# Routed experts in a hybrid decoder layer: 50 tiles of whole and half units with bounded gathers and plain scatters, in place of 72 tiles with scatter-adds

## The reference

```python
_, idx = lax.top_k(jnp.where(expert_mask, biased, -jnp.inf), TOP_K)   # 8 experts a token
w = w / jnp.sum(w, axis=-1, keepdims=True) * ROUTED_SCALE
...
def expert(acc, p):
    wg, wu, wd, g = p
    a = jax.nn.silu(t @ wg) * (t @ wu)
    return acc + g[:, None] * (a @ wd), None
```

## Time and profile before

| | |
|---|---|
| time, median of 3 runs (lowest to highest) | 2030.07 us (2028.19 to 2030.41) |
| the profiled execution's own time, and its span | 2028.67 us, 2026.8 us |
| mean granted TensorE clock | 0.968 |
| busy: PE, DVE, ACT, POOL | 93%, 32%, 22%, 20% |
| moved by DMA | 419.35 MB: 339.19 on q1 (SP), 78.10 on q0 (POOL) |

### The profile page before, as it was taken

The page is one execution under the profiler, slowest core; times in us unless marked ns, Lnnn a source line. Parts: engine busy times, 40 slices in busy tenths (PEclk is TensorE's granted clock), DMA queues, the critical chain, the costliest instruction groups (busy, mean ns, idle before and its releaser), DMA issues.

```text
span 2026.8 us, 25917 instructions
## 1 busy us (share of the span) xinstructions
PE 1890.4 (93%) x8348; PEld 1188.2 (59%) x8348; DVE 645.5 (32%) x1571; ACT 445.8 (22%) x946; POOL 411.0 (20%) x661
## 2 busy tenths in 40 slices
PE   5999789989998899999979899999999999999994
PEld 2844467567767668888766444444444444444443
DVE  1215841694269550001266311111111111111114
ACT  1204521452144430000021111111111111111112
POOL 0003420353034100000002322222222222222220
PEclk8999989999999999999978899999999999999997
DMA  9123332111210553210114699999999999999952
GB/s 391 42 83 124 136 126 83 42 45 45 83 43 4 214 204 125 94 72 9 42 41 182 253 371 365 373 367 368 372 363 373 355 381 359 375 367 368 373 165 95
DMA packets 56948, 419.35 MB, mean 207 GB/s; under 512 B 6289, under 2 KB 10001, under 8 KB 31145
## 3 DMA queue, kind: packets, MB, share of 16 engines
q1 hardware_dynamic: 33689, 339.19, 42.0%
q0 software_dynamic: 21456, 78.10, 14.7%
q10 hardware_dynamic: 1728, 1.05, 0.2%
HBM read 362.70 MB, written 55.61 MB: 206 GB/s over the span
## 4 chain that ended last, share of the span: by engine, by line
PE 80%; DVE 9%; ACT 5%; DMA 3%; issue 1%; POOL 1%; SPq 0%; POOLq 0%; DVEq 0%; ACTq 0%
PE ps L1039 25%; PE ps L1061 12%; PE ps L901 10%; PE ps L862 9%; PE ps L847 7%; PE ps L1030 3%; PE ps L933 3%; DVE work L1439 2%; ACT work L585 2%; PE ps L818 2%; ACT work L587 2%; DVE work L1428 1%; DMA Xb<-xT 1%; PE ps L1000 1%; DMA st_out<-work 1%
## 5 line engine op out<-in xcount | busy, mean ns | idle before, releaser
L1039 PE MATMUL ps<-W,work 128*128 128x512 f32 x1168 | 515.2, 594 | 1.6 <-ACT work L1223 1.2
L1039 PEld LDWEIGHTS ps<-W,work 128*128 128x128 f32 x1168 | 216.9, 191 | 247.7 <-issue 247.7
L1061 PE MATMUL ps<-work 128*128 128x512 f32 x576 | 259.1, 592 | 0.0
L1749 DVE SCALAR_TENSOR_TENSOR work<-ps,work 128x256 f32<-128x256 f32 x73 | 35.3, 484 | 515.1 <-ACT work L1229 515.1
L862 PE MATMUL ps<-Hb,W 128*128 128x260 f32 x768 | 172.8, 389 | 0.1
L1061 PEld LDWEIGHTS ps<-work 128*128 128x128 f32 x576 | 103.8, 190 | 103.3 <-issue 103.3
L862 PEld LDWEIGHTS ps<-Hb,W 128*128 128x128 f32 x768 | 148.4, 194 | 23.9 <-ACT work L1123 0.5
L1258 POOL TENSOR_TENSOR work<-work 128x128 f32<-128x128 f32 x168 | 82.8, 525 | 381.2 <-ACT work L587 380.8
L1759 DVE COPY work<-ps 128x512 f32<-128x512 f32 x144 | 99.7, 692 | 178.8 <-DMA ffrows<-work 91.9
L1328 POOL DMA_INDIRECT ffrows<-work x72 | 115.7, 1607 | 195.8 <-DVE work L1759 122.4
L847 PE MATMUL ps<-W,Hb 128*128 128x512 f32 (+1 forms) x320 | 138.4, 592 | 0.0
(11 more groups left out here) (255 smaller groups left out, 2232.1 us busy)
## 6 DMA issues: line engine op xcount, KB each, us to landing
W<-wexp SPq DMA_DIRECT2D x74, 2048.0 KB, 8.7
work<-wexp SPq DMA_DIRECT2D x73, 1024.0 KB, 8.0
W<-wq SPq DMA_DIRECT2D x36, 2048.0 KB, 8.0
work<-st_in SPq DMA_DIRECT2D x8, 1024.0 KB, 9.3
st_out<-work SPq DMA_DIRECT2D x8, 1024.0 KB, 7.5
Xb<-xT SPq DMA_DIRECT2D x2, 2080.0 KB, 18.2
h2rows<-work SPq DMA_DIRECT2D x5, 512.0 KB, 2.6
yT<-Xb SPq DMA_DIRECT2D x2, 1040.0 KB, 5.2
```

Source lines behind the costliest of these rows:

```text
L1039: mm = pe.matmul(ps[:, k % 2, :], xe[:, k % 2, c, :], GU[:, k % 4, c, :], start=(c == 0), stop=(c == KC - 1))
L1061: mm = pe.matmul(ps[:, 4 + hf, :], aT[:, k % 2, f, :], WD[:, k, f, hf * 512:(hf + 1) * 512], start=(f == 0), stop=(f == 1))
```

## The change

The reduction of the experts' results moves from the scatter to the last stage, and tiles can hold two experts.

- *Units.* An expert's slots are cut in units of 64. Two units of one expert are a whole tile; a left-over unit shares a tile with the left-over unit of another expert. The loop goes over pairs of tiles: the first (k = 0) of one expert, the second (k = 1) of two half units, each with its own weights. If there are more whole tiles than mixed ones, the surplus is put in the second list as two halves of one expert. By the counts of the reference's router there are 28 whole tiles and 43 left-over units, so the loop has max(22, (28 + 22) / 2) = 25 rounds, 50 steps, against 72.
- *Matmuls.* For a mixed tile `parts` makes two matmuls of each: 64 columns of stationary data with one expert's weights, and the other 64 with the other's. Transposes are the same.
- *Weights.* Three slots in place of four, one loaded for k = 0, two for k = 1; each is refilled when its own matmuls are done.
- *Gathers and scatters.* Two gather buffers in place of four, and gathers two tiles ahead in place of three. Both DMAs have a bound: rows whose index lies above it (those of empty slots) are not moved. The scatter writes each choice's row to its own place in `yrows` (4160 rows) and adds nothing.
- *Last stage.* For each tile of tokens SP loads 8 rows a token from `yrows` (4 MB a full tile), DVE multiplies each by its gate and adds it (`total`, 8 operations of 128x1024), and the residual (`residual`) comes one tile of tokens later.
- *Routing.* More small DVE operations count units and make two index lists; the gate values are picked after the lists. The shared expert's result stays in SBUF.
- *Merge stage.* `ORDER` puts one product before each state update.

```diff
-            for _ in range(2 if k % 3 == 0 else 1):
-                ORDER.append(decode.pop(0))
-        ORDER += [("N1", 0), ("P", 12), ("S", 0), ("N2", 0)] + [("P", k) for k in range(13, 4 * len(MERGE))]
+            ORDER.append(decode.pop(0))
+        ORDER += [decode.pop(0), ("N1", 0), ("P", 15), ("S", 0), ("N2", 0)] + [("P", k) for k in range(16, 4 * len(MERGE))]
...
             with sp.Fori(1, nq) as i:
-                for k in range(4):
-                    gate(sp, "sp", s_hh, i * 4 + (k + 2))
-                    load_tile(i * 4 + (k + 1), (k + 1) % 4, "gu", s_gu)
-                    gate(sp, "sp", s_y, i * 8 + (2 * k + 2))
-                    load_tile(i * 4 + k, k, "dn", s_dn)
...
+                gate(sp, "sp", s_hh, i * 2 + 3)
+                load_expert(i, 0, "gu", s_gu)
+                gate(sp, "sp", s_hh, i * 2 + 4)
+                for h in range(2):
+                    load_expert(i * 2 + (NLIST + h), 1 + h, "gu", s_gu)
+                gate(sp, "sp", s_y, i * 4 + 6)
+                load_expert(i, 0, "dn", s_dn)
+                gate(sp, "sp", s_y, i * 4 + 8)
+                for h in range(2):
+                    load_expert(i * 2 + (NLIST + h), 1 + h, "dn", s_dn)
...
+            def parts(k):
+
+                return [(slice(0, TS), 0)] if k == 0 else [(slice(0, UNIT), 1), (slice(UNIT, TS), 2)]
...
                 for c in range(KC):
-                    mm = pe.matmul(ps[:, k % 2, :], xe[:, k % 2, c, :], GU[:, k % 4, c, :],
-                                   start=(c == 0), stop=(c == KC - 1))
+                    for at, slot in parts(k):
+                        mm = pe.matmul(ps[at, k, :], xe[:, k, c, at], GU[:, slot, c, :], start=(c == 0), stop=(c == KC - 1))
...
             def gather(t, k, copied):
-                gate(pool, "pool", s_xt, t * 2 + 2)
+                gate(pool, "pool", s_xt, t * 2 + 6)
...
+                pool.indirect_dma_start(out=xg[k], out_offset=None, in_=h2rows,
+                                        in_offset=bass.IndirectOffsetOnAxis(ap=idg[0:TS, k:k + 1], axis=0),
+                                        bounds_check=NT - 1, oob_is_err=False).then_inc(s_ga[k], 16)
...
-                    gather(i * 4 + (k + 3), (k + 3) % 4, i * 8 + (2 * k + 4))
...
-                                            in_=yb[0:TS, k % 2, :], in_offset=None, compute_op=ALU.add).then_inc(s_add, 16)
...
+                    gather(i * 2 + (k + 2), k, i * 4 + (2 * k + 3))
...
+                                            in_=yb[0:TS, k, :], in_offset=None, bounds_check=YTRASH - 1, oob_is_err=False).then_inc(s_add, 16)
...
+                    dve.scalar_tensor_tensor(out=row, in0=picked[m % 3][0:rows, k * D:(k + 1) * D], scalar=gk[0:rows, t, k:k + 1],
+                                             in1=row, op0=ALU.mult, op1=ALU.add).then_inc(s_fs, 1)
...
+            for m in range(TT):
+                total(m)
+                if m:
+                    residual(m - 1)
+            residual(TT - 1)
```

More of the change, by code:

```diff
@@ L292, in decoder_step @@
         slotk = view(OB, 2520, TT * 8, "p (t k) -> p t k", t=TT)
[L293 to L297, removed]
+        pairs = view(OB, 2560, NE)
+        odd = view(OB, 2624, NE)
+        thr = view(OB, 2688, NE)
+        shift = view(OB, 2752, NE)
+        rounded = view(OB, 2816, NE)
+        idxt = view(OB, 2880, MAXT + 4)
+        pad = view(OB, 960, MAXT + 4)
+        less = view(OB, 1040, MAXT + 4)
+        less_i = view(OB, 1120, MAXT + 4).bitcast(I32)
+        order = view(OB, 2960, 2 * NE, "p (a e) -> p a e", a=2)
+        before = view(OB, 3088, 2 * NE, "p (a e) -> p a e", a=2)
+        assert 2880 + MAXT + 4 <= 2960 and 3088 + 2 * NE <= R0
         gsum = view(tiny, 32, TT)
-        ecol = view(tiny, 37, 1)
-        erow = tiny[0:1, 64:64 + MAXT + 4]
+        ecol = view(tiny, 37, 2)
+        n_pair, n_all, n_two, two_end, skip = (view(tiny, 40 + k, 1) for k in range(5))
+        over, quadn = view(tiny, 46, 1), view(tiny, 48, 1)
+        erow = tiny[0:1, 64:64 + 2 * NLIST]
         ui = ints[:, 0:TT * 8].bitcast(U32).rearrange("p (t k) -> p t k", t=TT)
@@ L758, in _ @@
[L758 to L767 removed]
+            sp.wait_ge(s_gk8, 1)
@@ new lines, in _ @@
+            sp.sem_inc(s_gu[0], 16)
+            gate(sp, "sp", s_add, nq * 32 + 32)
+            gate(sp, "sp", s_hh, nq * 2 + 5)
+            for m, t in enumerate(TAIL):
+                n = min(P, NT - t * P)
+                since(sp, s_acc, m - 2)
+                for h in range(2):
+                    sp.dma_start(picked[m % 3][0:n, h * 4096:(h + 1) * 4096],
+                                 yrows[t * P * TOPK:(t * P + n) * TOPK, :].rearrange("(t k) d -> t (k d)", k=TOPK)
+                                 [:, h * 4096:(h + 1) * 4096]).then_inc(s_f1[m % 3 * 2 + h], 16)
@@ L1334, in _ @@
+            for k in range(2):
+                gate(pool, "pool", s_ga[k], nq * 16 + 16)
         @block.vector
@@ L1722, in _ @@
                     n += 1
             dve.wait_ge(s_abp, 40)
[L1724 to L1729 removed]
+            val = ps[0:TS, 5, 0:MAXT]
+            step(dve.memset(pad[:, MAXT:MAXT + 4], 1.0))
@@ L1740, in _ @@
+            step(dve.tensor_copy(idy_i, less))
+            settled()
+            dve.tensor_copy(idx_i, idxt).then_inc(s_T, 1)
+            pick(gk, gates)
+            dve.sem_inc(s_gk8, 1)
             dve.sem_inc(s_a, 2)
```

361 lines of the change are left out of this document (203 added, 158 removed).

## The result

The changed kernel takes **2209.4 us** (median of four runs, 2206.5 to 2217.3) against 2030.2 us of the kernel before: ratio 1.089, 95% interval 1.086 to 1.092. Slower by 9%, where 1998 us was forecast. The profiled execution has a span of 2207.1 us (before 2026.8) and a mean granted clock of 0.893 (before 0.968).

A forecast was written before the change was run, and what follows sets the result against it. PE was taken to bound the kernel, with DMA some 14% spare. Loop -71, last stage +47, merge -7, routing +1 and last scatter -1 sum to -31 us on 2028.7: 1998 us forecast, range 1930 to 2060.

The forecast's parts named there:

- The new wait: Expert loop, ahead of each turn: PE waits for the gather, 8.88 us from turn to gather plus landing, 14.2 a step.
- the quiet case: Gather landing in the loop: 4.6 us where few other transfers ran, against 7.2 median inside the old loop; 5.3 taken.
- rival 2: Gather wait ahead of the turn: landing as in the loop before, 16.1 us a step, 2053 us, up to 2080; chance 0.26.
- The clock: Expert loop: PE's clock falls behind idle stretches in one step of four, 0.8 us a step on average, making 15.0.
- PE's 11.40: Expert loop: PE needs 11.40 us for a mixed step as for a whole one, 570 us for 50 steps.
- Rival 3: Mixed tiles' matmuls: the halves run one after the other, PE needs 33.3 us a round, 2080 us; chance 0.04.
- DMA's 12.8 us a step: Expert loop: DMA moves 10.8 MB a round at 423 GB/s, 25.5 us, or 12.8 a step.
- Rival 4: Expert loop's DMA: the HBM limit of 358 GB/s holds in the mix, 15.1 us a step, 2003 us; chance 0.03.
- Rival 5: Loop's gathers and scatters: bounds change nothing, rows of empty slots still move, 13.6 us a step for DMA, 2013 us; chance 0.04.
- The last stage: Behind the loop: 60 us from SP's load in place of 16.4, plus 3 for the means; +47 us, 40 to 55.
- The merge: Merge stage: two more products ahead of the awaited state remove most of 9 us of idle and slow PE; -7 us.
- Routing: Routing stage: about 24 more small DVE operations mostly covered, five more behind the tables; +1 us.

The follow-up runs named there:

- both orders were mended: Changed kernel with SP's refills in the order PE frees the slots and POOL's gather of t+3 ahead of the scatter of t: 1917.8 us, ratio 0.944.

## Why the prediction was wrong

- **The new wait: right in place and loop, wrong in its landing.** The step that failed is "So the gather is nearer to the quiet case: I take 5.3 us". It measured 9.8 on average; 4.5 us times 50 are up to 225 us (somewhat less, since the last steps, when few loads are left, are quicker), enough for the whole miss of 201 us in the loop (+129 in place of -72); the other 10 of the 211 are mostly the last stage and routing. Two errors are in the landing.
  1. *"That other refills are taken from three slots costs nothing more"*. I compared how long each slot is free and did not ask when SP gets to it. One wait out of PE's order moved 2 MB from an idle stretch of DMA into the burst around a gather. Mending it gives 88 us. My heavier burst was 5.2 MB; it is 8.4.
  2. *When a burst ends was taken for when the gather's rows move.* In the late gather the rows don't wait for the bytes ahead, they take turns with packets of 14 KB on average. Even with the refills in order the landing is 7.1 us, that of the loop before, and without refills 4.2; how much of the difference is turn-taking no run says. A landing like that of the loop before was rival 2, priced at 16.1 to 16.6 us a step; the measured step was 17.4, and 19.2 with the first error. "It decides from 15.6 up" held.
- **The clock** was 0.8 us a step; 9.6 against 8.5 us from turn to gather makes it 1.1, and 1.6 where every step idles 3 us or more. Not large by itself. In the changed kernel it falls mostly in the long steps, behind some 10 us of idleness, as it did behind 3.55 us at 712.59.
- **PE's 11.40** held but for 0.3 us a step. "The drain is not to be seen, and I charge nothing": it is to be seen once nothing else is waited for. Rival 3 is refuted.
- **DMA's 12.8 us a step** held within 4% (13.3) once both orders were mended. Rival 4: 408 GB/s in the mix against its 358; the trace does not bear that limit out for this core. Rival 5 (the bounds change nothing): wrong for bytes, but near the truth when DMA carries the loop, 12 us.
- **A cheaper issue of the plain scatter**, "up to 0.5 us": 8.5 against 8.9 from turn to gather. The issue itself is 0.59 us shorter, 1.01 in place of 1.60.
- **The last stage** was mis-sized: +54.5 against +47. An addition comes every 1.32 us (1.28 busy), not every 1.20 as drawn out from 260 columns; 40 times 0.12 is 4.8 us. The first came 4.1 us after the load, not 3. That is 5.9 of the 7.5 us; the rest I did not follow up. The means did come behind, at the lower clock.
- **The merge** was right in size, -6.4 against -7, and wrong in its reason. **Routing** was +2.5, not +1; which of its operations the 1.5 us are, I did not follow up.
- The range of 1930 to 2060 missed by 149 us at its upper end: both its slow cases took the old loop's landing as the worst.

## What to carry over

Before a buffer's lead is given up, write down the loop it closes (turn, down, copy, scatter, gather) and price the landing as that of a loaded queue; a gather put ahead of the scatter instead of behind it was worth 247 us here, with no more buffers. Check that a queue's waits stand in the order in which the resources come free, for one wait out of order leaves DMA empty and then floods it. And a small scattered transfer beside large plain ones is priced by its packets more than by its bytes: leaving rows out took no packet away here, and gave 12 us where DMA carried the loop and 51 where the gather was waited for.

## What I had not expected of the hardware

- A bounded indirect DMA still issues a packet for each row left out: 288 a tile for gather and scatter with or without bounds.
- The two DMA queues alternate packet for packet while both have work (63 to 62 in two microseconds, 14 KB packets against ones of 0.3 KB on average); a gather that lands in 4.2 us alone took 14 beside 8.4 MB of loads, 9 with 4 KB packets.
- Going between 128 and 64 columns costs TensorE some 0.15 us each time, 0.6 us a round; a pass with 8 moving columns took 0.23 us at the lower clock (1.85 us for 8), about what one with 128 takes (1.91 to 2.08). The weight loads beside them took 1.82 us for 8, so these may have set the pace. The transposes into 8 columns in the changed kernel took 1.02 us for 8 at the same clock.
- A scatter that accumulates takes DMA more time than its bytes say: from 1200 to 1600 us POOL's queue in the kernel before held 35.2% of the engines' time for 36.85 MB, with bare scatters and all rows moved 19.0% for 30.94 MB. No run changes the accumulation alone.
